# Six-layer transformer kernel on one core: x in four pieces, the first weight chunk in two, the relative bias wholly in the first MLP

## What is computed

```python
h = rms_norm(x, attn_norm[0]); x = x + mla_mixer(h, ...)      # stage "mla":  latent attention, rotary part, 8 heads
h = rms_norm(x, mlp_norm[0]);  x = x + sq_relu_mlp(h, ...)    # stage "mlp0": 1024 -> 4096 -> 1024, relu squared
h = rms_norm(x, attn_norm[1]); x = x + moba_mixer(h, ..., rel_bias_table)   # stage "moba": attention with a relative bias
h = rms_norm(x, mlp_norm[1]);  x = x + sq_relu_mlp(h, ...)    # stage "mlp1"
h = h + rms_norm_2(gdn_mixer(...), post_norm)                 # stage "gdn":  gated delta rule
h = h + rms_norm_2(fox_mixer(...), post_norm)                 # stage "fox":  attention with forget gates
```

## Time and profile before

| | |
|---|---|
| median of three runs | 936.48 us (933.59 to 937.98) |
| the profiled execution | 937.91 us |
| its span on the core | 936.2 us |
| PE busy in the span | 906.1 us (97%) |
| DVE, ACT, POOL busy | 625.1, 512.0, 110.4 us |
| DMA queue of SP | 141.82 MB |

### The profile page before, as it was taken

One profiled execution on the slowest core, in us unless ns is written; L12 is line 12 of the kernel. 1 busy time (PEld: TensorE's weight loads), 2 busy tenths in 40 slices (PEclk: granted clock), 3 DMA queues, 4 the chain that ended last, 5 costly groups with the idle time before them and its releaser, 6 DMA issues.

```text
span 936.2 us, 14470 instructions
## 1 busy us (share of the span) xinstructions
PE 906.1 (97%) x5944; PEld 815.6 (87%) x5944; DVE 625.1 (67%) x1035; ACT 512.0 (55%) x766; POOL 110.4 (12%) x144
## 2 busy tenths in 40 slices
PE   5898999999999999999999999999999999999997
PEld 5776899999998888899999998999998987798886
DVE  5798766566455686655454445898886776856884
ACT  5787454345354667544454453664446664747662
POOL 0055000000000000000000000007476612000000
PEclk9999999999999999999999999999899999999999
DMA  7442356275554633455645544562511302345431
GB/s 245 146 139 87 134 182 245 90 263 178 176 192 137 224 123 141 156 183 176 211 154 207 186 174 138 182 224 90 170 56 68 136 1 90 127 164 207 134 113 46
DMA packets 61681, 142.74 MB, mean 152 GB/s; under 512 B 5296, under 2 KB 7344, under 8 KB 61616
## 3 DMA queue, kind: packets, MB, share of 16 engines
q1 hardware_dynamic: 61616, 141.82, 44.4%
HBM read 140.76 MB, written 1.05 MB: 151 GB/s over the span
## 4 chain that ended last, share of the span: by engine, by line
PE 84%; POOL 4%; issue 4%; DVE 4%; ACT 2%; SPq 1%; DMA 0%; POOLq 0%; DVEq 0%; ACTq 0%
PE ps L480 81%; PE ps L488 4%; POOL arena L3379 3%; DVE wlo L2208 1%; POOL wlo L3379 1%; SPq L3513 1%; POOL arena L3429 1%; ACT arena L1354 1%; ACT whi L1354 0%; DVE arena L2208 0%; DMA pint<-rel_bias_table_dram 0%; DVE oth L2208 0%; DVE X L2208 0%; ACT otl L1354 0%; DVE arena L2211 0%
## 5 line engine op out<-in xcount | busy, mean ns | idle before, releaser
L2208 DVE TENSOR_TENSOR wlo<-raw,whi 128x2048 fp32r<-128x2048 f32 (+3 forms) x130 | 287.4, 2218 | 162.1 <-ACT whi L1354 162.0
L1354 ACT ACTIVATE whi<-raw 128x2048 fp32r<-128x2048 f32 (+3 forms) x136 | 251.1, 1853 | 264.1 <-PE ps L480 225.5
L480 PE MATMUL ps<-xh,whi 128*128 128x256 f32 (+2 forms) x784 | 224.3, 286 | 0.3 <-DVE wlo L2208 0.3
L480 PE MATMUL ps<-xl,whi 128*128 128x256 f32 (+2 forms) x784 | 222.7, 284 | 0.0
L480 PE MATMUL ps<-xh,wlo 128*128 128x256 f32 (+2 forms) x784 | 222.7, 284 | 0.0
L480 PE MATMUL ps<-whi,oth 128*128 128x512 f32 x384 | 151.7, 395 | 0.0
L480 PEld LDWEIGHTS ps<-xh,whi 128*128 128x128 f32 (+2 forms) x784 | 149.9, 191 | 1.6 <-DVE wlo L2208 0.4
L480 PEld LDWEIGHTS ps<-xl,whi 128*128 128x128 f32 (+2 forms) x784 | 149.9, 191 | 1.0
L480 PEld LDWEIGHTS ps<-xh,wlo 128*128 128x128 f32 (+2 forms) x784 | 149.8, 191 | 0.4
L480 PE MATMUL ps<-whi,otl 128*128 128x512 f32 x384 | 149.7, 390 | 0.0
L480 PE MATMUL ps<-wlo,oth 128*128 128x512 f32 x384 | 149.7, 390 | 0.0
(11 more groups left out here) (147 smaller groups left out, 1108.2 us busy)
## 6 DMA issues: line engine op xcount, KB each, us to landing
raw<-mlp_w_in_dram SPq DMA_DIRECT2D x32, 1024.0 KB, 5.2
raw<-mlp_w_out_dram SPq DMA_DIRECT2D x32, 1024.0 KB, 4.9
raw<-gdn_w_in_dram SPq DMA_DIRECT2D x16, 1024.0 KB, 5.3
raw<-moba_w_qkv_dram SPq DMA_DIRECT2D x12, 1024.0 KB, 5.1
raw<-kv_w_dram SPq DMA_DIRECT2D x8, 1024.0 KB, 5.3
raw<-fox_w_in_dram SPq DMA_DIRECT2D x8, 1024.0 KB, 5.4
raw<-mla_w_o_dram SPq DMA_DIRECT2D x4, 1024.0 KB, 5.1
raw<-moba_w_o_dram SPq DMA_DIRECT2D x4, 1024.0 KB, 6.1
```

The lines of the kernel that those rows point to most:

```text
L480: return eng.matmul(o, l, r, start=start, stop=True, skip_group_check=True)
L1354: return eng.activation(o, i, f, **kw)
L2208: return eng.tensor_tensor(o, a, b, f)
```

## The change

The edits by hand are these:

```diff
-    for k in range(0, 8, 2):
-        add("in", A["mla_w_in"], k, 2, 0, 704, st="mla", k0=k)
+    for k, n in ((0, 1), (1, 1), (2, 2), (4, 2), (6, 2)):
+        add("in", A["mla_w_in"], k, n, 0, 704, st="mla", k0=k)
...
-        s_c0, s_xin, ... = sem("s_c0"), [sem("s_xin0"), sem("s_xin1")], ...
+        s_c0, s_xin, ... = sem("s_c0"), [sem(f"s_xin{i}") for i in range(1, 4)], ...
...
-        BIAS_IN_MLA = 3
+        BIAS_IN_MLA = 0
...
                 if stage == "mla":
-                    L.wait_ge(s_c0, 32)
-                    L.wait_ge(s_xin[j2 // 2], 16)
+                    L.wait_ge(s_c0, 48)
+                    if j2:
+                        L.wait_ge(s_xin[j2 - 1], 16)
...
-            def x_in(ch):
-                c = slice(512 * ch, 512 * ch + 512)
-                eng.dma_start(X[:, :, c], ...).then_inc(s_xin[ch], 16)
+            def x_in(j2):
+                c = slice(256 * j2, 256 * j2 + 256)
+                eng.dma_start(X[:, :, c], ...).then_inc(s_xin[j2 - 1] if j2 else s_c0, 16)
...
             first_in()
+            x_in(2)
+            x_in(1)
             load(0)
-            x_in(1)
+            x_in(3)
+            load(1)
             x_in(0)
-            load(1)
-            small_in()
+            load(2)
+            small_in_a()
+            small_in_b()
+            load(3)
             tables_in()
-            load(2)
-            load(3)
             load(4)
```

`xhi`, `squares` and `constants_in` wait for 48 on `s_c0` too, which now counts `cst`, `cols` and the first fourth of x together. Chunks are numbered one higher from the second on (137 in all). Besides, all the order lists were planned again, so that steps stand in other places in every stage. In "mla" the bias steps are gone from PE and DVE, and their calls stand in "mlp0":

```diff
             turn_x("mla", 3)
-            to(1, 3)
-            bias_mm(0)
-            to(4, 0)
+            to(5, 0)
             turn_c(0)
...
             k_T(0, 1)
-            bias_mm(1)
-            bias_mm(2)
+            to(8, 3)
             q_T(0)
...
-            to(18, 0)
+            to(23, 0)
+            bias_mm(0)
+            bias_mm(1)
+            to(27, 0)
+            bias_mm(2)
             bias_mm(3)
```

More of the change, by code:

```diff
@@ L511, in quarter @@
                     x_ready(stage, d["k0"] // 2)
-                    for k in range(2):
+                    for k in range(d["a"]):
                         tok = mm3(P[b][:, 0:n], xh[:, d["k0"] + k, s], xl[:, d["k0"] + k, s], wh[:, k, a:a + n],
@@ L1389, in squares @@
                 if stage == "mla":
-                    for ch in range(2):
-                        L.wait_ge(s_xin[ch], 16)
+                    L.wait_ge(s_c0, 48)
+                    for s_ in s_xin:
+                        L.wait_ge(s_, 16)
                 else:
@@ L1684, in scalar_program @@
             hi(0)
+            hi(1)
             xhi("mla", 0)
@@ L1696, in scalar_program @@
             rsq("mla_x")
-            proj_scale()
             hi(5)
             hi(6)
+            proj_scale()
+            hi(7)
             c_hi(0)
@@ L2816, in vector_program @@
             lo(0)
+            gain("mla")
             xlo("mla", 0)
+            lo(1)
             xlo("mla", 1)
             xlo("mla", 2)
+            lo(2)
             xlo("mla", 3)
             read_positions()
-            lo(1)
-            bias_table()
-            bias_ind(0)
-            gain("mla")
-            lo(2)
+            lo(3)
             rope_angle()
             mean_x("mla")
-            bias_add(0)
-            lo(3)
-            bias_ind(1)
+            lo(4)
+            bias_table()
+            rsq_b("mla_x")
+            lo(5)
+            proj_scale()
             rope_cos()
-            rsq_b("mla_x")
-            rope_table()
-            proj_scale()
-            lo(4)
             c_lo(0)
             c_lo(1)
-            lo(5)
+            rope_table()
             c_mean()
+            lo(6)
+            rsq_b("mla_c")
             c_lo(2)
-            bias_ind(2)
-            rsq_b("mla_c")
             c_lo(3)
             c_lo(4)
-            lo(6)
             k_rope()
+            lo(7)
             k_sums(0)
-            lo(7)
+            lo(8)
             q_sums(0)
@@ L2854, in vector_program @@
             q_sums(1)
+            q_norm(0)
             kp_copy()
-            q_norm(0)
-            bias_add(1)
-            bias_add(2)
+            lo(9)
             rsq_b("mla_q1")
-            lo(8)
-            lo(9)
+            lo(10)
             q_norm(1)
@@ L2910, in vector_program @@
             lo(18)
-            bias_ind(3)
+            lo(19)
             hidden(0, 0, 0)
             hidden(0, 0, 1)
-            lo(19)
             lo(20)
-            bias_add(3)
-            bias_ind(4)
             lo(21)
-            bias_ind(5)
             lo(22)
+            bias_ind(0)
+            bias_ind(1)
             hidden(0, 1, 0)
+            hidden(0, 1, 1)
             lo(23)
-            bias_add(4)
-            gain("moba")
-            hidden(0, 1, 1)
+            lo(24)
+            bias_ind(2)
+            bias_ind(3)
+            bias_add(0)
             hidden(0, 2, 0)
-            lo(24)
+            lo(25)
+            lo(26)
             hidden(0, 2, 1)
-            bias_add(5)
-            lo(25)
-            bias_ind(6)
-            bias_ind(7)
-            lo(26)
-            bias_add(6)
+            bias_add(1)
             lo(27)
-            bias_ind(8)
-            bias_ind(9)
-            bias_add(7)
             hidden(0, 3, 0)
@@ L2942, in vector_program @@
             lo(30)
+            bias_add(2)
+            bias_add(3)
+            hidden(0, 3, 1)
+            bias_ind(4)
+            bias_ind(5)
+            level_masks()
+            gain("moba")
             lo(31)
-            hidden(0, 3, 1)
-            bias_add(8)
-            variance(0)
+            bias_add(4)
+            bias_ind(6)
             lo(32)
             lo(33)
-            bias_ind(10)
-            bias_ind(11)
-            level_masks()
-            bias_add(9)
             lo(34)
+            bias_add(5)
             lo(35)
+            bias_ind(7)
             hidden(0, 4, 0)
             hidden(0, 4, 1)
-            hidden(0, 5, 0)
-            bias_add(10)
+            bias_add(6)
+            bias_add(7)
             lo(36)
             lo(37)
-            bias_add(11)
-            hidden(0, 5, 1)
             lo(38)
             lo(39)
+            bias_ind(8)
+            bias_ind(9)
+            hidden(0, 5, 0)
             lo(40)
             lo(41)
+            bias_add(8)
+            hidden(0, 5, 1)
+            bias_ind(10)
+            bias_add(9)
+            bias_ind(11)
             lo(42)
@@ L2972, in vector_program @@
             hidden(0, 7, 1)
+            variance(0)
             lo(44)
             lo(45)
+            bias_add(10)
+            bias_add(11)
             lo(46)
+            lo(47)
             residual("mlp0", 0)
@@ L3053, in vector_program @@
             lo(70)
+            hidden(1, 1, 0)
+            hidden(1, 1, 1)
             lo(71)
@@ L3472, in gpsimd_program @@
             level(1, 1)
+            level(0, 1)
             select(6)
-            level(0, 1)
             select(7)
@@ L3646, in sync_program @@
             load(78)
+            load(79)
             load(80)
-            load(79)
             load(81)
@@ L3660, in sync_program @@
             load(92)
+            load(93)
             load(94)
-            load(93)
             load(95)
@@ L3667, in sync_program @@
             load(99)
+            load(101)
             load(100)
-            load(101)
             load(102)
@@ L3675, in sync_program @@
             load(107)
-            load(109)
             load(108)
             load(110)
+            load(109)
+            load(112)
             load(111)
```

761 lines of the change are left out of this document (381 added, 380 removed).

## The result

The changed kernel takes a median of 945.31 us in four runs (941.68 to 946.43), beside 937.09 us for the kernel before in four runs: ratio 1.0098, 95% interval 1.0075 to 1.012. **It is slower by about 1%, outside the range.** The forecast was 934.6 us.

A forecast was written before the change was run, and what follows sets the result against it. PE, busy 906.1 of 936.2 us, was taken as the bound, so only its idle time and clock could move. Terms summed to -1.9 us, giving 934.6 us against the 936.48 median; range 929.5 to 938.0.

The forecast's parts named there:

- x: At the start, PE's wait for x grows because x comes in shorter runs: +0.6 us, bounds 0 and +2.8.
- The estimate from the Trainium skill: At the start, descriptor overhead for 1 against 2 KB rows of x: +0.13 us, not taken into the sum.
- The first projection: PE's wait for the second chunk's low part goes (-0.74 us), and 24 bias matmuls leave (-0.77 us).
- The latent part: Before the first "kv" matmul, `c_lo(0)` starts sooner: -1.05 us; PE may stay at full clock: -0.8 us.
- The rest of the first attention: From 35 us on, 48 bias matmuls leave, part lost in POOL waits: -1.2 us, bounds 0 and -6.1.
- The first MLP: The 72 moved bias matmuls are paid in full there: +2.1 us; DVE's part costs nothing.
- DVE in the MLP: Rival: bias in six pairs overdraws DVE in the first MLP, PE waits six times: +6.6 us, 941.2 us; chance 0.06.
- Elsewhere: All other stages, where lists are only reordered: 0, bounds -1.5 and +1.5 us.
- follows steps that are the same: Half clock from 660 us, 3.0 us lost, stays in the sum because the thin matmuls ahead stay put.
- The clock: Rival: half clock at 35 and 660 us vanishes, -5.8 us, 930.7 us; chance 0.15.
- Slower by over 0.5%: Outcome above 941.2 us for the whole kernel; chance 0.05.

The follow-up runs named there:

- e9: Kernel before with all twelve bias blocks in the first MLP and all engines' lists there from the changed kernel: 938.63 us, 1.0037.
- e12: Changed kernel with the row-sum steps in "gdn" in the local order of before on PE, POOL and DVE: 937.92 us, 1.0021.
- e3: Kernel before, with the changed kernel's order lists from the second MLP on: 941.35 us, 1.0068.
- e2: Changed kernel up to the second MLP, the order lists of before from there on: 937.80 us, 1.0027.
- e16: Kernel before with new start and latent order, first x and half chunk loaded first, two resulting waits on first bias and late loads addressed: 938.36 us, 1.0027.
- e14: Kernel before with only `q_square(5)` moved behind the low part on POOL: 941.41 us, 1.0058.
- e1: The changed kernel again, unedited: 946.19 us, 1.0117.
- e10: Kernel before with the new start, the first "kv" chunk's low part ahead of `proj_scale` and `c_lo` ahead of the rotation table on DVE: 935.26 us, 0.9995.
- e13: Kernel before with only PE's `sums(1)` to `sums(3)` as late as in the changed kernel: 938.57 us, 1.0024.
- e5: Changed kernel with `q_square(5)` ahead of POOL's low part and PE's `sums(1)` and `sums(3)` where they were before: 942.05 us, 1.007.

## Why the prediction was wrong

- *x:* +0.6 forecast, +0.82 in the first pair of traces. The start moves by itself: 9.35 to 9.97 us in six traces with the old order of SyncE, 9.86 to 10.67 in nine with the new one. The means are 0.66 apart. Right in size and in its choice of rows. The estimate from the Trainium skill, "DMA: Bandwidth & Descriptors", was +0.13: the means are not with it.
- *The first projection:* -0.74 and -0.77. Right: no wait between the 24th and 25th matmul, and the first projection ended 19.3 us after the start (31.09 less the wait of 1.34 and less 10.44; forecast 19.5).
- *The latent part:* -1.05 forecast. The wait for `xl` fell from 1.43 to 0.43 us, and the matmul came at 33.07 us, forecast 33.1. These terms make -1.96 together, and 2.02 were measured. That PE stayed at full clock behind it was taken half, as no row told which; in the profiled execution it did, and POOL began its rotation 3.6 us sooner than before.
- *The rest of the first attention:* -1.2 forecast; idle time rose by 1.95 us. **This term failed in its sign.** Of the lead of 3.6 us at POOL's start, 1.5 went into the longer rotation and 1.7 into the half clock behind the second wait, and 0.4 was left at the first residual. The prediction had the covering in it ("they were its cover") and the point that would prove it wrong (idle time above 4.75 us), but its bounds stopped at 0: "all of it ends in longer waits". It counted the bias steps that leave DVE as time won for POOL. What it missed is that DVE's low parts move up into their place, beside POOL's steps, which then take longer. By its ratio e9 puts the whole move of the bias at +0.37% (3.5 us); the three terms for it (-0.77, -1.2, +2.1) add up to +0.1.
- *The first MLP:* +2.1 forecast, +1.8 by the residuals (189.8 us from the first of the rows `X<-ps,X` to the first of `X<-ps,st,X`, 188.0 before). Right. The rival "DVE in the MLP" did not happen.
- *Elsewhere:* "the profile gives no reason for a sign: 0, bounds -1.5 and +1.5". **This is the step that failed most.** The new order in "gdn" cost about 8 us (e12 against the changed kernel), and the new lists of the second half cost 6.4 us by themselves (e3). The order of the changed kernel was at hand and had the row: on POOL one square behind a low part of 5.4 us. A bound from the idle time that is there cannot see a wait that a reordering makes. That the half clock at 660 us "follows steps that are the same" was wrong as well: the thin sums had been moved apart.
- *The clock* was taken as something that could only be won back. It was lost: the mean clock of an execution is 0.987 to 0.993 in the changed kernel and 0.993 to 1.0 in the kernel before, and about 6 of the 9.5 us between their means are the clock's, in places that changed from run to run.

Slower by over 0.5% was given a chance of 0.05, by a rival (DVE, bias in pairs) whose mechanism was not the one that decided.

What stays open: why the clock falls behind a wait in one execution and not in another of the same kernel, and why it takes more from e2, e12 and e16 than from the kernel before. The low parts beside POOL's rotation were not moved by themselves, and e16's last wait was not taken away.

## What to carry to other kernels

When PE is busy 97% and the lists of the engines are written again as a whole, go through every place where one short step was moved behind a long one on an engine that feeds PE, in all stages, and price each at its wait and at least as much again for the clock (a wait of 2.4 us stands in e14, which lost 5.0 us, and in e3, which lost 6.4). Work that is removed from ahead of a wait is worth nothing until what ends the wait is sooner too, and costs where it is put instead. Taking steps out of one engine's list pulls the next ones forward: look at what they then run beside. Steps that depend on each other over three lists must be moved back together: one or two of them gave 4 us, all three 8.

## What the runs showed of the hardware that was not expected

- A wait of PE of 2.3 to 2.4 us between full matmul streams was followed by 3 to 14 us at the 1.2 GHz level in some traces (e1, e3, e14) and by none behind the wait at 56 us in the first trace of the changed kernel. The wait of 2.3 us for the second rotated q is followed by that level in e3, e9 and e10 and not before, in e13 and in e14. Executions of one kernel differ by up to 5.7 us (941.68 and 947.41) with these waits equal to 0.02 us. Such a stretch can also come with next to no wait ahead of it: at 660 us before PE had been idle for 0.14 us in the ten us ahead.
- The same first stage, instruction by instruction (before, e13 and e14), reached its first residual at 106.4, 104.5 and 104.3 us: the first with half clock at 35 us, the two others without. (0.2 to 0.3 us of that is a sooner x.)
- The same steps on POOL take longer when DVE makes a low part beside them: 4.42, 5.63 and 7.03 to 7.16 us for twelve steps with 0, 1.5 and 2.7 to 2.8 us of low parts. A square on POOL takes 0.61 us in e5 (at 653.73) and 3.83 us in e14, where this step of DVE stands beside it:

```profile
646.64 2.28 DVE L2208 TENSOR_TENSOR wlo<-raw,whi 128x2048 fp32r<-128x2048 f32 x1
```

- SyncE needs 8.4 us to issue 16 transfers of 1 to 4 KB, 0.35 to 0.7 us each. Their 40 KB at the 231 GB/s of the start would be 0.2 us by an estimate.
